# The delta rule's chunks in three streams instead of two, and two places of the array for the last level of the triangular inverses

## The chip, the cores and the metric

The kernel runs on one core of a Trainium2 chip. Its engines take their instructions from queues of their own, each in order: PE (TensorE, matmuls and the weight loads before them), DVE (VectorE), ACT (ScalarE), POOL (GpSimd) and SP, which only issues DMAs here. They meet at semaphores. The metric is the time of one execution on the device, in microseconds (us). All arithmetic is float32; in the trace one matmul of 128 rows shows as two records, a transpose as one.

## What is computed

The reference runs three blocks of a sequence model, one after another, on 512 tokens of width 1024. The change lies in the first block's mixer, and in a helper that the third block also uses. The mixer, cut to what matters:

```python
def chunk_gated_delta_rule(q, k, v, g, beta):
    """S_t = exp(g_t) S_{t-1} (I - beta_t k_t k_t^T) + beta_t k_t v_t^T ; o_t = S_t^T q_t."""
    ...
    m = jnp.where(strict, jnp.einsum("bhncd,bhnmd->bhncm", kb, kc) * decay, 0.0)
    t_sys = jnp.eye(CHUNK, dtype=q.dtype) + m
    u = lax.linalg.triangular_solve(t_sys, vb, left_side=True, lower=True, unit_diagonal=True)
    w = lax.linalg.triangular_solve(t_sys, kb * jnp.exp(gc)[..., None], left_side=True,
                                    lower=True, unit_diagonal=True)
    a_qk = jnp.einsum("bhncd,bhnmd->bhncm", qc, kc) * decay
    def step(state, xs):
        v_new = u_i - jnp.einsum("bhcd,bhde->bhce", w_i, state)
        o_i = ...   # q_i * exp(g_i) @ state + a_i @ v_new
        state = state * jnp.exp(g_last)[..., None, None] + jnp.einsum("bhcd,bhce->bhde", k_dec, v_new)
        return state, o_i
...
o = rms_norm(o, gdn_norm_g) * jax.nn.silu(z.reshape(b, l, GDN_HEADS, GDN_DV))
y_a = o.reshape(b, l, GDN_VW) @ w_gdn_out
```

There are 8 heads of width 128. The third block has an RWKV layer in two directions, which the kernel also computes in chunks with inverses of the same kind.

## The kernel before

The kernel cuts the 512 tokens into `NT = 4` chunks of 128 and handles all 8 heads of a chunk together, in two halves of 4 heads: one PSUM bank holds 4 heads of 128 columns. For each chunk c there are three parts of work.

- The **front**, the first part of `pe_gdn_prepare`, `act_gdn_prepare` and `dve_gdn_prepare`. Six decay matmuls of 512 columns (L1260: `dec`, `eb`, `bb`, for two halves) spread gates over the tile, ScalarE takes their exponentials (L1303), VectorE masks them (L1332 to L1338). Then eight groups of four matmuls or transposes, `gdn kind` 0 to 3 for each half (L1282, L1286), which VectorE takes out with one product each (L1347 to L1353).
- The **inverse** of the unit triangular 128 x 128 matrix of every head (`pe_inverse`, `act_inverse`, `dve_inverse`), by doubling blocks: levels of block size 2 to 32 have a group `inv x` (L833), a transpose `inv t` (L818) that ScalarE copies, and a group `inv y` (L849), each of 16 matmuls of 64 x 64 in all four places of the array; VectorE masks and subtracts (L930, L939). The last level, 64, has an `inv x` of 8 matmuls at one place (L861), 16 transposes by the identity (L869) and an `inv y` of 8 at one place (L878); ScalarE copies all three results (L896, L901, L906). VectorE starts the inverse with four masked products and a subtraction (L914, L919).
- The **steps** (`pe_gdn_steps` and its like), which carry the state from chunk to chunk: `gdn ks` (L1379), two VectorE operations, `gdn vn` (L1391), a copy by ScalarE, `gdn o` (L1402, L1403), `gdn ds` (L1412), and the state's update by VectorE. The second half of the heads stands behind the first.

These parts are generators, and the order of every queue is the order in which a driver advances them. `mixed` puts front and inverse of chunk 0 between the pieces of the conv output gemm (L272, four matmuls a piece), one step for every second piece. `gdn_rounds` then advances `steps(c)` and `prepare(c + 1)` in turn; since an inverse is longer than the steps, most of it stands alone. After the last chunk follow the squares of the output (ScalarE, L1118), the head sums over them (`pe_head_sums`, L628), the first pair of z's gemm (`pe_pair`) and the seven-product steps of z, ga, the output and the mix (`pe_seven`, L348), for which VectorE forms sums of the input (`dve_halves`, L411) and of the weights (L397).

`banks` deals the eight PSUM banks in turn, `weights` the four weight buffers `w0` to `w3` of 1 MB; SP loads a buffer when the last matmul that read it is done. During the delta rule `w0` to `w2` hold the kept tiles of odd chunks and `w3` holds `vn_at` and `R1`, so no weights are loaded there.

The RWKV layer of the third block runs sixteen inverses in `rw_rounds`, each between the work of three other streams.

## Time and profile before

| | us |
|---|---|
| median of 3 runs | 4777.89 |
| lowest, highest | 4777.67, 4782.76 |
| the profiled execution | 4782.63 |
| its span in the trace | 4780.8 |

The profile shows one execution. Its busy times tell how long each engine worked, not what set the end: a wait of an engine counts only where the work behind it is on the chain that ends last. TensorE has two levels of clock, 2.4 GHz (a granted clock of 1.00 in the rows) and 1.2 GHz (0.50); a mean in between is a mix in time. In a timeline a row merges instructions of one line; its duration runs to the end of the last one, which overlaps the next row's start, so from start to start is the better price.

### The profile page before, as it was taken

The numbers are of one execution on the slowest core, as the hardware profiler recorded it, in microseconds if no ns is written. First come the engines' busy times: TensorE is split into PE (matmuls) and PEld (weight loads), VectorE is DVE, ScalarE is ACT, GpSimd is POOL, SyncE is SP. The second block draws the span as 40 slices with busy tenths as digits, with TensorE's granted clock in tenths as the row PEclk, the third lists the DMA queues.
The fourth block names the chain that finished last, engine by engine and source line by source line (L and its number), as shares of the span: only waits on it lengthen the run. The fifth ranks groups of instructions, "written<-read, shape, count | busy, mean of one in ns | idle before, by whom it ended". The sixth has DMA issues, their size and how long they took to land.

```text
span 4780.8 us, 65963 instructions
## 1 busy us (share of the span) xinstructions
PE 4470.1 (94%) x28828; PEld 3314.3 (69%) x28828; DVE 2535.4 (53%) x4388; ACT 824.3 (17%) x1473; POOL 153.9 (3%) x260
## 2 busy tenths in 40 slices
PE   8999998968999899799998999998999988999899
PEld 7887444556878688656655648885888777777644
DVE  5674866333643546546244425555646537777501
ACT  0001012211011100221122210001100014444210
POOL 0000000000000000000000000000000003222100
PEclk9998999967999999899999999998989999999999
DMA  6533452002322222111211122222222210000021
GB/s 240 176 101 58 68 73 53 10 1 56 95 88 80 71 88 82 60 54 36 69 40 36 44 62 90 87 71 88 80 70 89 71 49 2 3 3 2 28 92 44
DMA packets 284958, 311.75 MB, mean 65 GB/s; under 512 B 7168, under 2 KB 277632, under 8 KB 281600
## 3 DMA queue, kind: packets, MB, share of 16 engines
q1 hardware_dynamic: 284672, 307.55, 22.5%
q8 instruction: 227, 3.72, 0.3%
q14 instruction: 59, 0.48, 0.0%
HBM read 305.43 MB, written 2.10 MB: 64 GB/s over the span
## 4 chain that ended last, share of the span: by engine, by line
PE 49%; DVE 4%; ACT 2%; issue 1%; DMA 0%; DVEq 0%; ACTq 0%; SPq 0%
PE ps L348 19%; PE ps L272 13%; PE ps L2940 1%; PE ps L2125 1%; PE ps L317 1%; PE ps L833 1%; PE ps L849 1%; PE ps L818 1%; PE ps L1845 1%; PE ps L2665 1%; PE ps L1834 1%; PE ps L2860 1%; PE ps L2849 0%; PE ps L471 0%; ACT main L901 0%
## 5 line engine op out<-in xcount | busy, mean ns | idle before, releaser
L272 PE MATMUL ps<-main,w 128*128 128x512 f32 (+1 forms) x2832 | 1243.9, 596 | 21.9 <-DMA w<-in_ffn_wg 12.2
L348 PE MATMUL ps<-main 128*128 128x256 f32 x5136 | 1139.2, 379 | 0.0
L348 PEld LDWEIGHTS ps<-main 128*128 128x128 f32 x5136 | 975.5, 190 | 133.1
L272 PEld LDWEIGHTS ps<-main,w 128*128 128x128 f32 x2832 | 543.2, 195 | 647.2 <-issue 619.1
L348 PE MATMUL ps<-main,w 128*128 128x256 f32 x3872 | 863.9, 379 | 1.4 <-DVE main L416 1.4
L348 PEld LDWEIGHTS ps<-main,w 128*128 128x128 f32 x3872 | 736.1, 190 | 105.8 <-issue 4.3
L435 DVE TENSOR_TENSOR main<-main,ps 128x512 f32<-128x512 f32 x164 | 112.8, 688 | 417.7 <-PE ps L348 417.5
L661 DVE SCALAR_TENSOR_TENSOR main<-main,params_sb 128x512 f32<-128x512 f32 x256 | 192.5, 752 | 9.1
L387 ACT COPY main<-ps 128x256 f32<-128x256 f32 x98 | 36.5, 372 | 896.3 <-PE ps L348 896.3
L432 DVE TENSOR_TENSOR main<-main,ps 128x512 f32<-128x512 f32 x98 | 67.3, 687 | 221.2 <-PE ps L348 218.4
L440 DVE TENSOR_TENSOR main<-main,ps 128x512 f32<-128x512 f32 x164 | 112.8, 688 | 78.0 <-PE ps L348 76.7
L397 DVE TENSOR_TENSOR main<-w 128x512 f32<-128x512 f32 (+1 forms) x164 | 111.1, 678 | 31.1 <-DMA w<-in_w_in 12.2
L400 DVE TENSOR_TENSOR main<-main,w 128x512 f32<-128x512 f32 (+1 forms) x164 | 112.4, 685 | 5.7
L402 DVE TENSOR_TENSOR main<-w,main 128x512 f32<-128x512 f32 (+1 forms) x164 | 112.4, 685 | 5.6
L3166 POOL MEMSET w<- 128x512 f32 x128 | 60.8, 526 | 1643.3 <-ACT main L2709 1333.6
L398 DVE TENSOR_TENSOR main<-w 128x512 f32<-128x512 f32 (+1 forms) x164 | 111.1, 677 | 0.0
L387 ACT COPY tmp<-ps 128x256 f32<-128x256 f32 x66 | 24.6, 372 | 498.9 <-PE ps L348 498.9
L2179 DVE TENSOR_TENSOR main<-main 128x512 f32<-128x512 f32 x56 | 38.8, 692 | 135.3 <-PE ps L2125 127.0
L533 ACT ACTIVATE tmp<-main 128x512 f32<-128x512 f32 x104 | 63.8, 629 | 266.2 <-DVE main L585 79.0
L432 DVE TENSOR_TENSOR main<-tmp,ps 128x512 f32<-128x512 f32 x66 | 45.3, 687 | 110.1 <-PE ps L348 109.1
L317 PE MATMUL ps<-w,main 128*128 128x256 f32 (+1 forms) x512 | 101.6, 355 | 0.0
L3092 DVE COPY_PREDICATED w<-consts_sb,ps 128x512 f32<-128x512 uint32 x128 | 85.8, 724 | 27.2 <-PE ps L2940 25.9
(457 smaller groups left out, 4809.7 us busy)
## 6 DMA issues: line engine op xcount, KB each, us to landing
w<-in_w_in SPq DMA_DIRECT2D x58, 1024.0 KB, 6.8
w<-in_e_w_in SPq DMA_DIRECT2D x28, 1024.0 KB, 5.1
main<-in_ada_w SPq DMA_DIRECT2D x24, 1024.0 KB, 5.0
w<-in_ffn_wg SPq DMA_DIRECT2D x22, 1024.0 KB, 6.4
w<-in_ffn_wu SPq DMA_DIRECT2D x22, 1024.0 KB, 6.4
w<-in_o_w_in SPq DMA_DIRECT2D x20, 1024.0 KB, 5.4
w<-in_ffn_wd SPq DMA_DIRECT2D x16, 1024.0 KB, 5.1
w<-in_w_up SPq DMA_DIRECT2D x16, 1024.0 KB, 5.7
```

The source lines that it names most:

```text
L272: i = pe.mm(PS[b][:, 0:n], wv[:, k, f * 128:(f + 1) * 128], g.X(kg + k), start=kg + k == 0, stop=kg + k == g.nk - 1)
L317: i = pe.mm(PS[b][:, 0:m], g.X.ap[:, k, t * 128:(t + 1) * 128], wv[:, k, :], start=k == 0, stop=k == g.nk - 1)
L348: t = pe.mm(PS[b][:, 256 * half:256 * half + 256], weight[:, m, :], x(m), start=m == 0, stop=m == n - 1)
L397: v.tt(S[0], a21, a22, ADD).then_inc(v.inc(s, "sum 0", *step), 1)
L398: v.tt(S[2], a21, a11, SUB).then_inc(v.inc(s, "sum 2", *step), 1)
L400: v.tt(S[1], S[2], a22, ADD).then_inc(v.inc(s, "sum 1", *step), 1)
L402: v.tt(S[3], a12, S[1], SUB).then_inc(v.inc(s, "sums", *step), 1)
L432: v.tt(outer, two(first), b[1], ADD).then_inc(v.inc(s, "out", "seven", 1, *step), 1)
L435: v.tt(inner, two(c[3]), b[2], ADD).then_inc(v.inc(s, "most", *step), 1)
L440: v.tt(inner, inner, b[3], ADD).then_inc(v.inc(s, "out", "seven", 3, *step), 1)
L661: v.stt(out, src[:, j:j + TOK], w(j), out, MUL, ADD).then_inc(v.inc(s, "tap", j, *step), 1)
L3092: v.pick(c3(MS[hd](kind)), mid(const(mask), 4).bitcast(U32), c3(bank("rw ms", i, k))).then_inc(v.inc(s, "out", "rw ms", i, k), 1)
```

## The change

- `gdn_rounds` now drives three streams: the steps of chunk c, the inverse of chunk c + 1 and the front of chunk c + 2 (`together`, `behind`). The halves of the heads in the steps are streams of their own. Rounds: steps 0 with front 1; inverse 1 with front 2; steps 1, inverse 2, front 3; steps 2, inverse 3 and a filler; steps 3.
- The filler is the first pair of z (`pe_pair(pe, G_z, 0)`, slowed by `slowly`) on PE and the input sums (`dve_halves`) on VectorE. `vn_at` and `R1` move out of `w3`, so z's weights can be loaded there early; the tiles of the input sums and of z move too.
- The squares and head sums of a half chunk follow its `gdn o` at once, into a bank held for them (bank 7).
- The inverses' start moves from VectorE to GpSimd (`pool_gdn`).
- Around the conv output gemm, `beside` puts one step of the front behind every third piece and one step of the inverse behind every piece. The kinds of the front come in the order of `g_order`.
- In `pe_inverse` the last `inv x` and `inv y` write to two places in turn, in two banks each; the last transposes are split into a late half (beside `inv x`) and an early half. VectorE copies `inv x` and half of the last `inv y`; ScalarE keeps the rest. This also holds for the RWKV layer.

```diff
@@ drivers @@
+def behind(turns, steps):
+    for _ in range(turns):
+        yield
+    yield from steps
+def together(*streams):
+    streams = list(streams)
+    while streams:
+        streams = [g for g in streams if next(g, "end") != "end"]
+        yield
+def slowly(steps, turns):
+    for _ in steps:
+        for _ in range(turns):
+            yield
+def beside(aside, *parts):
+    for steps, every in parts:
+        for k, _ in enumerate(steps):
+            if k % every == 0:
+                next(aside, None)
     run(aside)
@@ pe_inverse, last level @@
-        for e in range(2):
-            for n in range(4):
-                i = 4 * e + n
-                t = pe.mm(PS[b][late, 64 * i:64 * i + 64], MT[early, i, late], D4[early, n, e, :], start=True, stop=True)
...
-        for i in range(8):
-            for (b, _), h in zip(two, HALF):
-                t = pe.mm(PS[b][h, 64 * i:64 * i + 64], D4[h, i % 4, i // 4, :], ident[h, h], start=True, stop=True)
+        places = late, early
+        for n in range(4):
+            for e in range(2):
+                i = 4 * e + n
+                t = pe.mm(PS[x_banks[e][0]][places[e], 64 * n:64 * n + 64], MT[early, i, late], D4[early, n, e, :],
+                          start=True, stop=True)
+            if n == 3:
+                t.then_inc(pe.inc(s, "mm", "inv x", 64, *name), 1)
+            for e in range(2):
+                i = 4 * e + n
+                t = pe.mm(PS[late_bank][late, 64 * i:64 * i + 64], D4[late, n, e, :], ident[late, late], start=True, stop=True)
...
+        for i in range(8):
+            t = pe.mm(PS[early_bank][early, 64 * i:64 * i + 64], D4[early, i % 4, i // 4, :], ident[early, early],
+                      start=True, stop=True)
...
-        pe.wait_ge(*at("out", "inv t", 64, *name))
-        for i in range(8):
-            t = pe.mm(PS[b][early, 64 * i:64 * i + 64], x[late, 64 * i:64 * i + 64], full[late, i, late], start=True,
-                      stop=True)
+        pe.wait_ge(*at("out", "inv t", 64, "late", *name))
+        places = early, late
+        for n in range(4):
+            for e in range(2):
+                i = 4 * e + n
+                t = pe.mm(PS[y_banks[e][0]][places[e], 64 * n:64 * n + 64], x[late, 64 * i:64 * i + 64], full[late, i, late],
+                          start=True, stop=True)
@@ dve_inverse, last level @@
-        yield
+        v.wait_ge(*at("mm", "inv x", 64, *name))
+        for e, h in enumerate((late, early)):
+            v.move(x[late, 256 * e:256 * e + 256], bank("inv x", 64, e, *name)[h, 0:256]).then_inc(
+                v.inc(s, "out", "inv x", 64, e, *name), 1)
+        v.also("out", "inv x", 64, *name)
+        yield
+        v.wait_ge(*at("mm", "inv y", 64, *name))
+        if free:
+            v.wait_ge(*at(*free))
+        v.ts(full[early, 4:8, late], bank("inv y", 64, 1, *name)[late, 0:256].rearrange("p (i b) -> p i b", b=64), -1.0, None,
+             MUL).then_inc(v.inc(s, "out", "inv y", 64, 1, *name), 1)
@@ delta rule @@
-    vn_at, R1 = wv8[6], wv8[7]
+    vn_at, R1, g_sq = (mem(26864 + 1024 * i, 8, 128) for i in range(3))
+    g_turns = ((0, 1), (3, 4), (2, 5))
+    g_order = [(0, 0), (1, 0), (0, 1), (1, 1), (0, 2), (1, 2), (0, 3), (1, 3)]
+    def pool_gdn(p):
+        s = sem["pool", "gdn"]
+        after(p, "ln1")
+        for c in range(NT):
+            for half in range(2):
+                p.wait_ge(*at("out", "gdn kind", c, half, 0))
+            if c:
+                p.wait_ge(*at("mm", "inv y", 2, "gdn", c - 1))
+            for quarter in QUARTERS:
+                start_blocks(p, s, ("gdn", c), g_mt[c % 2].ap, g_d1, True, [quarter])
+                p.wait_ge(*at("inv first", "pool", "gdn", c))
+            start_inverse(p, s, ("gdn", c), g_d1)
-    def gdn_rounds(e, prepare, steps):
+    def gdn_rounds(e, front, inverse, steps, fill=iter(())):
         after(e, "gdn first")
-        for c in range(NT):
-            for _ in zip_longest(steps(e, c), prepare(e, c + 1) if c < NT - 1 else iter(())):
-                pass
-            e.fence("gdn", c)
+        both = lambda c, late: together(steps(e, c, 0), behind(late, steps(e, c, 1)))
+        run(together(both(0, 0), front(e, 1)))
+        run(together(inverse(e, 1), front(e, 2)))
+        if e.name == "dve":
+            dve_gdn_gate_row(e, 3)
+        run(together(both(1, 0), inverse(e, 2), behind(4, front(e, 3))))
+        if e.name == "pe":
+            banks.only(range(2, 7))
+        run(together(both(2, 0), inverse(e, 3), behind(5 if e.name == "dve" else 3, fill)))
+        run(together(both(3, 0), fill))
         e.fence("gdn")
     def pe_gdn(pe):
         banks.only(range(2, 8))
-        mixed(pe_gdn_prepare(pe, 0), pe_gemm(pe, G_cout), 2)
+        beside(pe_gemm(pe, G_cout), (pe_gdn_front(pe, 0), 3), (pe_gdn_inverse(pe, 0), 1))
...
+        weights.only((3,))
+        gdn_rounds(pe, pe_gdn_front, pe_gdn_inverse, pe_gdn_steps, slowly(pe_pair(pe, G_z, 0), 2))
@@ pe_mixers @@
-        for i in range(8):
-            pe_head_sums(pe, "o1", b, i, t512[i], ("o square", i))
-        run(pe_pair(pe, G_z, 0))
         for g, j in mixer_steps():
...
             run(pe_seven(pe, g, j))
+            if g is G_z and j == 2:
+                weights.only(range(4))
+                input_here("after gdn")
```

How PE's queue changes at the first inverse that stands in the rounds (chunk 1). Before, the end of front 1 and the first levels; L1282 and L1286 are kinds, L818 `inv t`, L833 `inv x`, L849 `inv y`:

```order
L1282 MATMUL ps<-main 128x128 x8
L1286 MATMUL ps<-consts_sb,main 128x128 x8
L818 MATMUL ps<-consts_sb,main 128x128 x4
L833 MATMUL ps<-main 64x64 x16
L849 MATMUL ps<-main 64x64 x16
L833 MATMUL ps<-main 64x64 x16
L818 MATMUL ps<-consts_sb,main 128x128 x4
L849 MATMUL ps<-main 64x64 x16
```

After, the same inverse; L846 is `inv t`, L861 `inv x`, L877 `inv y`, L1299 decay matmuls and L1313 kinds 0 and 1 of front 2:

```order
L846 MATMUL ps<-consts_sb,main 128x128 x4
L1299 MATMUL ps<-main,consts_sb 128x512 x2
L861 MATMUL ps<-main 64x64 x16
L1299 MATMUL ps<-main,consts_sb 128x512 x2
L877 MATMUL ps<-main 64x64 x16
L1330 MATMUL ps<-main,consts_sb 128x8
L1331 MATMUL ps<-main,consts_sb 128x8
L1313 MATMUL ps<-main 128x128 x4
L861 MATMUL ps<-main 64x64 x16
L846 MATMUL ps<-consts_sb,main 128x128 x4
L1313 MATMUL ps<-main 128x128 x4
L877 MATMUL ps<-main 64x64 x16
```

Between every two groups of the inverse now stands a group of front 2. PE's queue in the fourth round (steps 2 done, inverse 3), where L299 is a piece of z's pair in `w3`:

```order
L877 MATMUL ps<-main 64x64 x16
L299 MATMUL ps<-main,w 128x512 x4
L861 MATMUL ps<-main 64x64 x16
L846 MATMUL ps<-consts_sb,main 128x128 x4
L877 MATMUL ps<-main 64x64 x16
L299 MATMUL ps<-main,w 128x512 x4
L861 MATMUL ps<-main 64x64 x16
```

A piece stands behind `inv y`; nothing stands between `inv t` and `inv y`. SP's queue around the end of the delta rule, with what each load waits for: before

```order
L456 DMA w3<-in_w_in 128x8x256 [waits dve_gdn,pe_dense,act_gdn,pe_gdn]
L456 DMA w0<-in_w_in 128x8x256 [waits pe_dense]
L456 DMA w1<-in_w_in 128x8x256 [waits pe_dense]
L456 DMA w2<-in_w_in 128x8x256 [waits pe_dense]
```

and after:

```order
L483 DMA w3<-in_w_in 128x8x256 [waits pe_dense] x2
L483 DMA w3<-in_w_in 128x8x256 [waits dve_gdn,pe_dense,act_gdn,pe_gdn]
L483 DMA w0<-in_w_in 128x8x256
L483 DMA w1<-in_w_in 128x8x256
L483 DMA w2<-in_w_in 128x8x256
```

The first two loads (z's pair and its seven-product step for pair 2) no longer wait for the delta rule; the third is for pair 4 and goes to the same buffer, ahead of the loads to `w0`, `w1` and `w2`.

## Rows read from the trace of the kernel before

**Rows 1.** The profile's page: span, PE's busy time, one DMA row

```profile
span 4780.8 us, 65963 instructions
...
PE 4470.1 (94%) x28828; PEld 3314.3 (69%) x28828; DVE 2535.4 (53%) x4388; ACT 824.3 (17%) x1473; POOL 153.9 (3%) x260
...
w<-in_w_in SPq DMA_DIRECT2D x58, 1024.0 KB, 6.8
```

**Rows 2.** Stretches: length, busy us by engine (x records), granted clock, DMA share, GB/s

```profile
855.50:939.40 83.90, 79.24 (x596) 41.94 (x597) 24.04 (x49) 8.92 (x16) 0.00 (x0) 1.00 0.00 1
939.40:963.50 24.10, 16.86 (x112) 13.41 (x113) 15.95 (x28) 6.00 (x11) 0.00 (x0) 0.93 0.00 0
963.50:994.00 30.50, 21.78 (x405) 18.04 (x405) 5.35 (x21) 4.67 (x8) 0.00 (x0) 0.50 0.01 2
994.00:1027.80 33.80, 23.33 (x145) 18.45 (x145) 18.96 (x32) 6.61 (x12) 0.00 (x0) 0.85 0.00 1
1142.10:1170.30 28.20, 27.53 (x96) 18.94 (x97) 11.61 (x22) 7.65 (x12) 0.00 (x0) 0.76 0.67 150
939.40:1170.30 230.90, 170.89 (x1772) 136.70 (x1773) 83.33 (x179) 43.83 (x76) 0.00 (x0) 0.68 0.09 19
3950.00:4500.00 550.00, 498.29 (x9754) 404.80 (x9758) 412.98 (x1049) 245.59 (x444) 134.90 (x211) 0.98 0.02 4
```

**Rows 3.** PE's timeline, first inverse in the rounds: start, duration, work, [wait, releaser]

```profile
963.52 1.09 PE L818 MATMUL ps<-consts_sb,main 128*128 128x128 f32 x4 [7.15 <-DVE main L919]
...
968.77 1.13 PE L833 MATMUL ps<-main 64*64 64x64 f32 x32 [0.61 <-DVE main L939]
...
971.71 1.14 PE L849 MATMUL ps<-main 64*64 64x64 f32 x32 [0.77 <-ACT main L892]
973.44 1.13 PE L833 MATMUL ps<-main 64*64 64x64 f32 x32 [0.59 <-DVE main L939]
```

**Rows 4.** PE's timeline at full clock: inverse and conv gemm, decays, kinds

```profile
904.43 0.69 PE L833 MATMUL ps<-main 64*64 64x64 f32 x32 [0.61 <-DVE main L939]
905.05 0.66 PE L818 MATMUL ps<-consts_sb,main 128*128 128x128 f32 x4
905.54 3.60 PE L272 MATMUL ps<-main,w 128*128 128x512 f32 x8
...
942.50 1.02 PE L1260 MATMUL ps<-main,consts_sb 128*128 128x512 f32 x2
943.36 1.05 PE L1412 MATMUL ps<-w,main 128*128 128x128 f32 x8
...
953.55 1.95 PE L1282 MATMUL ps<-main 128*128 128x128 f32 x16
955.34 1.04 PE L1286 MATMUL ps<-consts_sb,main 128*128 128x128 f32 x8
```

**Rows 5.** PE's timeline behind the last chunk: head sums, three products

```profile
1142.77 12.27 PE L628 MATMUL ps<-consts_sb,tmp 128*128 128x1 f32 x64 [1.34 <-ACT tmp L1118]
...
1170.33 5.34 PE L348 MATMUL ps<-main,w 128*128 128x256 f32 x24
```

**Rows 6.** DMA issues from 1140 to 1166 us, median us to landing

```profile
w<-in_w_in SPq DMA_DIRECT2D x4, 1024.0 KB, 16.1
```

**Rows 7.** PE's timeline, RWKV stage: column halves in turn, last `inv y`

```profile
4195.89 1.15 PE L2980 MATMUL ps<-main,w 128*64 128x64 f32 x32
...
4200.26 1.11 PE L878 MATMUL ps<-main 64*64 64x64 f32 x16 [0.36 <-ACT main L901]
```

**Rows 8.** VectorE's timeline: inverse's start, a kind's product, a wait

```profile
894.99 1.76 DVE L914 TENSOR_TENSOR main<-main,consts_sb 64x256 f32<-64x256 f32 x4
...
956.10 0.68 DVE L1347 TENSOR_TENSOR main<-ps,main 128x512 f32<-128x512 f32 x1
...
4240.43 0.75 DVE L3103 SCALAR_TENSOR_TENSOR main<-tmp,params_sb,ps 128x512 f32<-128x512 f32 x1 [5.33 <-PE ps L2860]
```

**Rows 9.** GpSimd's timeline: the same start in the RWKV stage

```profile
3945.42 4.39 POOL L914 TENSOR_TENSOR main<-w,consts_sb 64x256 f32<-64x256 f32 x4 [19.66 <-DVE w L3092]
```

More of the change, by code:

```diff
@@ L2 @@
 from contextlib import ExitStack
-from itertools import zip_longest
+from itertools import chain
 import concourse.bass as bass
@@ L1047, in pe_mixers @@
         pe_gdn(pe)
-        b, before = banks.take("head sums", "o1")
-        if before:
-            pe.wait_ge(*at("out", *before))
-        for i in range(8):
-            pe_head_sums(pe, "o1", b, i, t512[i], ("o square", i))
-        run(pe_pair(pe, G_z, 0))
         for g, j in mixer_steps():
@@ L1296, in act_gdn_prepare @@
         if c > 1:
-            after(a, "gdn", c - 2)
-        for half in range(2):
-            hs = slice(4 * half, 4 * half + 4)
-            for which, step, lhs, fn in halves_of:
+            for half in range(2):
+                after(a, "gdn", c - 2, half)
+        for turn in g_turns:
+            for n in turn:
+                half = n // 3
+                hs = slice(4 * half, 4 * half + 4)
+                which, step, lhs, fn = halves_of[n % 3]
                 dst = {"dec": dec, "eb": EB, "bb": BB}[step]
+                if c and step != "eb":
+                    a.wait_ge(*at("out", "gdn kind", c - 1, half, 1))
                 a.wait_ge(*at("mm", "gdn " + step, c, half))
@@ new lines, in dve_gdn_beta_row, with dve_gdn_decays @@
+    def dve_gdn_beta_row(v, c):
+        if c > 1:
+            for half in range(2):
+                after(v, "gdn", c - 2, half)
+        v.wait_ge(*at("beta"))
+        v.tt(g_kept[c % 2][0].ap, bc(be[:, c, :], 128), mid(ident, 8), MUL).then_inc(
+            v.inc(sem["dve", "gdn"], "gdn row", c, 1), 1)
+    def dve_gdn_decays(v, c, half):
+        s, hs = sem["dve", "gdn"], slice(4 * half, 4 * half + 4)
+        v.wait_ge(*at("out", "gdn dec", c, half))
+        v.tt(dec.ap[:, hs, :], dec.ap[:, hs, :], mid(const("le"), 4), MUL).then_inc(v.inc(s, "gdn decay", c, half), 1)
@@ new lines, in act_gdn_steps @@
+    def act_gdn_steps(a, c, half):
+        s = sem["act", "gdn"]
+        ts_ = slice(c * 128, (c + 1) * 128)
+        hs = slice(4 * half, 4 * half + 4)
+        if c:
+            yield
+            a.wait_ge(*at("mm", "gdn o", c - 1, half))
+        a.wait_ge(*at("mm", "gdn vn", c, half))
+        a.copy(vn_at.ap[:, hs, :], c3(bank("gdn vn", c, half))).then_inc(a.inc(s, "out", "gdn vn", c, half), 1)
+        yield
+        a.wait_ge(*at("mm", "gdn o", c, half))
+        a.copy(O1.ap[:, hs, ts_], c3(bank("gdn o", c, half))).then_inc(a.inc(s, "out", "gdn o", c, half), 1)
+        a.fence("gdn", c, half)
+        if c:
+            a.wait_ge(*at("mm", "head sums", "o1", c - 1, half))
+        a.wait_ge(*at("out", "gdn o", c, half))
+        a.act(g_sq.ap[:, hs, :], O1.ap[:, hs, ts_], ACT.Square).then_inc(a.inc(s, "o square", c, half), 1)
+        yield
@@ L1315, in dve_gdn_prepare, with dve_gdn_steps @@
+    def dve_gdn_steps(v, c, half):
         s = sem["dve", "gdn"]
@@ L2872, in dve_shifted @@
         v.stt(out, PP.ap[:, f, o:o + 512], par("o_mu_3", 25 * d + f), out, MUL, ADD).then_inc(v.inc(s, *step), 1)
-    def behind(turns, steps):
-        for _ in range(turns):
-            yield
-        yield from steps
-    def together(*streams):
-        streams = list(streams)
-        while streams:
-            streams = [g for g in streams if next(g, "end") != "end"]
-            yield
     def rw_rounds(e, head, body, inverse, chain, tail, aside):
```

467 lines of the change are left out of this document (246 added, 221 removed).

## Prediction

> **What bounds the kernel now.** I read the page first: TensorE is busy 94% of 4780.8 us [rows 1], so only a stretch where it waits or runs at half clock can give much. The table of stretches shows where that is [rows 2]. From 939.4 to 1170.3 us, the delta rule's rounds and what follows them up to the first seven-product step of z, PE is busy 170.89 of 230.90 us at a granted clock of 0.68; around it the clock is 1.00. The stretch is a chain of phases that stand one after another. 939.4 to 963.5 is steps of chunk 0 with the fronts of chunk 1. 963.5 to 994.0 is an inverse alone. 994.0 to 1027.8 is steps and front again; the pair of phases repeats for the later chunks, the last chunk's steps stand alone, and 1142.1 to 1170.3 is head sums and the first pair of z.
>
> In the PE's timeline the inverse shows why it is slow [rows 3]. It begins after 7.15 us without PE work, in which VectorE works off the products of the front, and the granted clock falls to 0.50 there and stays for the whole inverse. One level, from one `inv x` to the next, takes 4.67 us (968.77 to 973.44), of which the waits for ScalarE's copy and VectorE's subtraction are 0.77 and 0.59. The same groups at full clock take 0.62 and 0.5 us from start to start (904.43 to 905.05 to 905.54) [rows 4]. So the inverse loses twice: nothing lies in its waits, and its matmuls run at 1.2 instead of 2.4 GHz.
>
> **The change, part by part.** *Work that stays.* Prices at full clock, from start to start [rows 4]: a decay matmul takes 0.86 (942.50 to 943.36); a kind 0 or 1 group 0.9 (1.95 for two); a kind 2 or 3 group 0.44 (1.04 for two, with the tail); four matmuls of a dense pair 3.44 (3.60 with overlap). A front is 6 x 0.86 + 0.3 + 4 x 0.9 + 4 x 0.44 = 10.8. An inverse is ten groups of 0.62, five transposes of 0.5, 1.9 for the last `inv x` with its transposes and 0.6 for the last `inv y`: 11.2. The steps of a chunk are groups of 0.9: 5.4 for chunk 0, 9.0 for chunks 1 and 2, 7.2 for the last. The head sums took 12.27 us [rows 5], mostly at half clock (0.76 over 1142.1 to 1170.3) [rows 2]; at full clock I take half, 6.1. The z pair is 4 x 3.44 = 13.8. Together 3 x 10.8 + 3 x 11.2 + 30.6 + 6.1 + 13.8 = 116.5 us of PE work for the stretch that takes 230.9 now.
>
> *What still waits.* I walked the five new rounds in the engines' order, with the hand-offs of rows 3 (about 0.6 us by VectorE, 0.77 by ScalarE) and 0.6 for each VectorE product of 512 columns (0.68 with its overlap) [rows 8]. Round 1 (steps 0 with front 1): the first inverse now starts by GpSimd; its four products take 4.39 us for what VectorE did in 1.76 [rows 8, 9], and with the subtraction I take 5.9 for the start. It begins when both kind 0 products are out of VectorE. PE has issued them after 5.4 of steps, 1.5 of head sums, 5.2 of decays, 0.3 and 1.8, so 14.2 us in; VectorE takes the second out behind two mask products, about 16.5 us into the round, while PE has 4 us of groups left: 22.5 us, 3.5 of it PE waiting. Round 2 (inverse 1 with front 2): each wait of a level has a decay pair or a kind group in it; 21.9 of work, 1.5 of waits: 23.5. Round 3 (steps 1, inverse 2, front 3): 9 + 11.2 + 10.8 + 1.6 of head sums = 32.6 of work, and 3 for the two additions before `gdn vn` and the chunk's copies: 35.5. Round 4 (steps 2, inverse 3, z pair): 9 + 11.2 + 13.8 + 1.6 = 35.6 of work; a chunk of z covers VectorE's wait but nothing stands between transposes and `inv y`, so 5 x 0.77 stay: 40. Round 5 (steps 3 alone): 7.2 + 1.6, and 1.6 of waits: 10.4. Sum 132. The squares and head sums of all but the last chunk, the z pair and the input sums then lie inside these. I add 5 us for orders of VectorE that I did not resolve and for short falls of the clock, as in the later stage of the same build (0.98 over 3950 to 4500 us, PE busy 498 of 550) [rows 2]: 137. **Gain 230.9 - 137 = 94 us.**
>
> *Before the rounds.* 855.5 to 939.4 holds 79.24 of PE work in 83.90 us [rows 2]. With a chunk of the conv gemm behind every step of the inverse, its waits close; the last level now stands uncovered, about 1 us. I take 5 of the 5.7 that the work leaves as **gain 5 us**. GpSimd's start there lies behind three gemm chunks (10 us) and costs nothing; without that cover it would cost 3.
>
> *First seven-product step.* z's weights for pair 2 land in `w3` during the rounds, so the step starts right after the last head sums. But pair 4 now goes to `w3` too, and SP can issue it, and the three behind it, only when pair 2's sixth product is done, some 7 us in (three products take 5.34, so four take 7.1) [rows 5]. Four loads issued together took 16.1 us in the median from issue to landing [rows 6]; this one is first of its four, and the median of all 58 loads of `w_in` is 6.8 [rows 1]. PE wants it 14 us in. At 6.8 it costs nothing, at 16.1 some 9 us; nearest is the single load: **loss 1 us**.
>
> *The last level.* `inv y` 64 has 8 matmuls at one place of the array, 1.11 us for 16 records; in two places at once I take the rate of L2980, which alternates the column halves: 1.15 for 32 records, so 0.67 for 16 with the tail of 0.2 [rows 7]. The last `inv x` with its transposes keeps about 1.9 us, since 16 of the transposes' records stay at one place and then 16 at another. But `inv y` waits 0.36 less [rows 7]: what it needs is copied while the last transposes run. That is 0.8 us in each of 16 inverses of the later RWKV stage, where PE is 91% busy [rows 2]. VectorE gets three more short operations there; it stands idle 5.33 us right at that point, waiting for the PE group behind `inv y` [rows 8], so they are covered; without that cover they would cost about 1 us each round. Two more banks per inverse shift all later banks; bounds from -13 to +5. **Gain 11 us.** The inverses of the delta rule are in their sum above.
>
> L2980 holds all rows of the array in use, alternates only the columns, and runs at 0.03 us a record against 0.06 for L878 [rows 7]; so I take the halved price. A rule speaks against it: the Trainium skill, "TensorE: Matmul & The Clock Gate", Part 3, "The mechanism", says that a weight load overlaps matmuls in flight only when its row group differs. The new `inv y` keeps one row group; by that rule it stays at 1.11 us and the gain here is 4 instead of 11.
>
> **Sum.** 5 + 94 - 1 + 11 = 109. The profiled execution took 4782.6 us, 4.7 over the median of the runs; 4782.6 - 109 = 4673.6, so 4669 for the median.
>
> **The rivals.**
> (a) *VectorE's order takes over.* In rounds 2 and 3 it has 17 and 23 us of work; each of 20 hand-offs of the inverses now stands behind a product of 0.68 that may itself wait for PE. If each costs one: 14 us less gain, 4683. For it: the queue is in order. Against: VectorE is free a quarter to a third of the time, and in the RWKV stage of the same kind PE waits little.
> (b) *The clock stays at half from round 2 on.* In the profile one wait of 7.15 us was followed by the whole phase of 30.5 us at 0.50 [rows 2, 3]. The wait for GpSimd in round 1 is 3.5 us by my walk, and twice that if it starts late. The 98 us of PE work in rounds 2 to 5 would take 98 more, less some 10 of waits that it fills: +88, 4757. Against: the RWKV stage has the same small matmuls among others and keeps 0.98, and here the work is dense.
> (c) *The streams do not overlap.* If a wait of one stream holds the queue of all (the fence on chunk c - 2, a bank still unread), the walls stay and only head sums, z pair and the last level move: about 28 + 5 + 10 gained, 4735. The queue order puts no such wait ahead of its producer, so little for it.
> (d) *Slower.* PE runs at half clock from the conv gemm to the end of z's pair, since small matmuls now stand everywhere between dense chunks. The 79 + 117 us of work would take 392, against 315 before: 109 - 196 = 87 us lost, 4865. It decides from the point where more than 109 of those 196 us of work run at half. Against: the same mix of inverse and gemm runs at 1.00 in 855.5 to 939.4 [rows 2].
> (e) *Two places in one row group don't run at once.* Then the last `inv y` stays at 1.11 us, 0.44 more than I take, in 16 inverses: 7 us less gain, 4676. L2980 speaks against it [rows 7]. (This is what the Trainium skill's rule in "TensorE: Matmul & The Clock Gate", Part 3, would give.)
>
> **How the numbers follow.** Chances: my sum 0.68, (a) 0.14, (b) 0.06, (c) 0.04, (d) 0.01, (e) 0.07. The forecast is 4669. Low end: of the waits only 2 us stay, and none of the 5 that I added (118.5 in place of 137): 4650. High end: (a) with the 9 us of the load and the last level at its bad bound (16 us less) gives 4708; beyond lie (b), (c) and (d), 0.11. Faster by over 0.2% (10 us, about what a measurement of this kernel can tell from no change): 0.98; within: 0.01; slower: 0.01.
>
> **What would show it.** Table of stretches: from the first `gdn vn` to the first seven-product step of z some 137 us at a clock over 0.9, conv gemm stretch 79. A wait of PE on GpSimd's L955 of 2 to 4 us once; PE's level of an inverse near 3.5 us. The last `inv y` at 0.6 to 0.7 us, and the RWKV stretch some 11 us shorter. I am wrong if the clock there is near 0.7, if the largest waits in the rounds are PE on VectorE's products, or if PE waits on the landing of `w3` by over 3 us.

## The result

| | before | after |
|---|---|---|
| median, us | 4778.11 (4 runs) | 4705.45 (4 runs) |
| lowest, highest | 4777.67, 4782.76 | 4703.34, 4711.52 |
| span of the profiled execution | 4780.8 | 4703.3 |

The ratio is 0.9845 with a 95% interval of 0.9833 to 0.9856: the change gains 73 us. The prediction was 4669, a gain of 109 from the median; the time lies in its range, near the high end, 36 us above the forecast.

The profile's page of the changed kernel (compare [rows 1]): PE is busy 45 us less, and the products that read weights now wait 5.3 us for a landing of `w_in`.

```profile
span 4703.3 us, 66069 instructions
...
PE 4425.1 (94%) x28828; PEld 3272.7 (70%) x28828; DVE 2557.4 (54%) x4444; ACT 808.2 (17%) x1453; POOL 171.0 (4%) x280
...
L375 PE MATMUL ps<-main,w 128*128 128x256 f32 x3872 | 866.0, 380 | 6.7 <-DMA w<-in_w_in 5.3
...
w<-in_w_in SPq DMA_DIRECT2D x58, 1024.0 KB, 6.3
```

Stretches of the changed kernel, with the columns of [rows 2] (length, busy us of PE, PEld, DVE, ACT, POOL, granted clock, DMA share, GB/s). First the conv gemm; the five rounds one by one and together, up to z's first seven-product step; the steps of z and ga behind it; a later stage that no edit touches; and the RWKV layer from the first to the last L3105, the PE group that stands behind the last `inv x` of every round (L2983 before).

```profile
855.56:936.27 80.71, 78.84 (x596) 41.21 (x597) 25.00 (x52) 8.13 (x15) 4.16 (x5) 1.00 0.07 14
936.27:960.13 23.86, 21.65 (x133) 17.51 (x133) 14.71 (x27) 8.33 (x15) 4.89 (x5) 0.93 0.00 1
960.13:986.50 26.37, 23.88 (x465) 18.10 (x465) 18.03 (x41) 6.67 (x12) 4.19 (x5) 0.94 0.01 2
986.50:1025.86 39.36, 36.43 (x566) 30.07 (x565) 22.86 (x53) 12.12 (x22) 4.17 (x5) 0.96 0.01 2
1025.86:1068.68 42.82, 37.87 (x535) 26.81 (x533) 17.85 (x49) 7.60 (x13) 0.00 (x0) 1.00 0.11 24
1068.68:1079.65 10.97, 9.64 (x84) 9.18 (x81) 3.10 (x5) 3.98 (x7) 0.00 (x0) 1.00 0.03 10
936.27:1079.65 143.38, 129.47 (x1773) 101.67 (x1773) 76.54 (x174) 38.70 (x69) 13.24 (x15) 0.96 0.04 9
1079.65:1193.30 113.65, 108.35 (x520) 95.57 (x520) 60.20 (x95) 15.12 (x21) 0.00 (x0) 0.97 0.46 102
3450.80:3470.67 19.87, 12.51 (x97) 10.85 (x96) 9.15 (x13) 5.63 (x9) 0.00 (x0) 1.00 0.00 0
3870.06:4407.76 537.70, 480.93 (x9512) 389.04 (x9508) 417.90 (x1052) 226.19 (x413) 132.86 (x208) 0.97 0.01 3
```

The last two of these stretches in the kernel before:

```profile
3529.90:3558.80 28.90, 21.53 (x98) 18.76 (x96) 9.25 (x13) 5.63 (x9) 0.00 (x0) 0.57 0.00 0
3958.48:4483.44 524.96, 478.98 (x9513) 389.58 (x9509) 397.20 (x1010) 237.39 (x427) 133.00 (x208) 0.99 0.01 3
```

The rounds take 143.38 us at a clock of 0.96, where the kernel before took 230.90 at 0.68 [rows 2]. That is the gain, and nearly all of what was forecast. But the RWKV layer, with the same number of PE records within one, takes 12.7 us more. And 9.0 us of the whole gain lie in a stage that the change does not touch: 3529.9 to 3558.8 before and 3450.8 to 3470.7 after hold the same instructions, once at a clock of 0.57 and once at 1.00.

### The profile page after: what moved, and what is told of

Read it like the earlier page. It is cut to its first block, busy times and chain, and to the rows that moved or that the text cites. A ratio compares the mean times of both kernels' runs of the same rounds, so it can differ in the third digit from the quotient of the medians.

```text
span 4703.3 us, 66069 instructions
## 1 busy us (share of the span) xinstructions
PE 4425.1 (94%) x28828; PEld 3272.7 (70%) x28828; DVE 2557.4 (54%) x4444; ACT 808.2 (17%) x1453; POOL 171.0 (4%) x280
## 4 chain that ended last, share of the span: by engine, by line
PE 50%; DVE 4%; ACT 1%; issue 1%; DMA 0%; DVEq 0%; ACTq 0%; SPq 0%
PE ps L375 20%; PE ps L299 14%; PE ps L2258 1%; PE ps L3062 1%; PE ps L344 1%; PE ps L861 1%; PE ps L846 1%; PE ps L877 1%; PE ps L498 1%; PE ps L1978 1%; PE ps L2798 1%; PE ps L1967 1%; PE ps L2993 1%; PE ps L2982 0%; DVE tmp L3005 0%
## 5 line engine op out<-in xcount | busy, mean ns | idle before, releaser
L299 PE MATMUL ps<-main,w 128*128 128x512 f32 (+1 forms) x2832 | 1242.7, 595 | 22.3 <-DMA w<-in_ffn_wg 12.3
L299 PEld LDWEIGHTS ps<-main,w 128*128 128x128 f32 x2832 | 541.3, 194 | 644.1 <-issue 615.1
L344 PEld LDWEIGHTS ps<-w,main 128*128 128x128 f32 x512 | 91.3, 201 | 14.0 <-issue 4.5
```

What stands on the lines that cost most here:

```text
L299: i = pe.mm(PS[b][:, 0:n], wv[:, k, f * 128:(f + 1) * 128], g.X(kg + k), start=kg + k == 0, stop=kg + k == g.nk - 1)
L344: i = pe.mm(PS[b][:, 0:m], g.X.ap[:, k, t * 128:(t + 1) * 128], wv[:, k, :], start=k == 0, stop=k == g.nk - 1)
```

## Where the time went, stretch by stretch

Each stretch is cut at the same instruction in every kernel: the first `gdn vn`; z's first seven-product step; the first product with ga (L1263, L1223 before); the first and the last L3105; the end. Lengths of before in us, and differences from them for the changed kernel and the ten that I ran (profiled executions).

| kernel | to first vn | rounds | z, ga | stages between | RWKV | rest | span |
|---|---|---|---|---|---|---|---|
| before | 939.4 | 230.9 | 104.8 | 2683.3 | 525.0 | 297.4 | 4780.8 |
| after | -3.1 | -87.5 | +8.7 | -6.5 | +12.7 | -1.8 | -77.5 |
| forecast | -5 | -94 | +1 | 0 | -11 | 0 | -109 |
| rw_add_later | -3.9 | -84.6 | +8.6 | -6.3 | -11.4 | -7.2 | -104.8 |
| rw_x_act | -4.0 | -84.6 | +8.6 | -6.3 | -13.2 | -5.5 | -104.9 |
| rw_old_last | -3.3 | -84.3 | +10.6 | -8.2 | -0.1 | +1.9 | -83.4 |
| z_w0 | -3.0 | -87.6 | +1.8 | -6.3 | +12.8 | -1.8 | -84.1 |
| y_in_turn | -3.7 | -84.2 | +7.4 | -12.6 | -10.4 | -1.3 | -104.8 |
| dve_start | -1.4 | -84.1 | +1.8 | -6.6 | -12.4 | -5.6 | -108.4 |
| best1 | -5.0 | -90.6 | +1.8 | -12.8 | -12.6 | -6.0 | -125.2 |
| gate_only | -4.9 | -90.6 | +8.9 | -6.2 | +9.4 | -1.8 | -85.2 |
| best2 | -4.0 | -90.5 | +1.8 | -12.3 | -11.3 | -7.2 | -123.5 |
| bef_last_x_act | -0.2 | -7.6 | 0.0 | -2.2 | -10.8 | -5.3 | -26.2 |

Read the columns down before you read a row across. "RWKV" has three levels: before's own, 10 to 13 us under it, and 9 to 13 over it; the edits say which. "Stages between" holds no edit of any kernel and still moves by 2 to 13 us. PE's idle time there is 144 to 146 us in all twelve kernels and only its busy time moves (2537 us before, 2531 in the changed kernel, 2525 in best1), for the same instructions: that is the granted clock, as in the stage at 3529.9 above, and a whole time can't be read closer than that. The kernel before itself had medians of 4778.1 to 4782.7 us beside the four groups of runs.

"Rest" is no stage without an edit throughout: it begins with the end of the last RWKV round, whose `inv y` stands behind the last L3105. From there to the next L2993 (L2860 before) it is 17.5 us before, 21.8 in the changed kernel and 15.5 in rw_add_later; behind that point 279.9, 273.7 and 274.7. The lengths of stretches decide below, and the whole times are given beside them.

## The RWKV layer: an addition in VectorE's queue

The timelines of one even and one odd round tell the layer's 12.7 us. In an even round of the changed kernel, the last `inv y` (L917) on PE takes 0.68 us for 16 records and starts right behind L3105; VectorE had copied `inv x` (L981) while PE was in the transposes:

```profile
4006.76 1.09 PE L3105 MATMUL ps<-w,main 128*64 128x128 f32 x16
4007.78 0.68 PE L917 MATMUL ps<-main 64*64 64x64 f32 x16
```

```profile
4005.91 0.87 DVE L981 COPY main<-ps 64x256 f32<-64x256 f32 x2 [0.86 <-PE ps L892]
```

That is the case that the prediction priced: 1.11 and a wait of 0.36 before [rows 7], 0.68 and none now. From the start of L3105 to that of the group behind `inv y` it is 1.64 us, where before had 2.49; the round gains 0.85. In the odd round behind it, PE and then VectorE:

```profile
4039.30 1.09 PE L3105 MATMUL ps<-w,main 128*64 128x128 f32 x16
4042.74 1.12 PE L917 MATMUL ps<-main 64*64 64x64 f32 x16 [2.34 <-issue]
```

```profile
4040.45 0.69 DVE L3272 TENSOR_TENSOR main<-main,ps 128x512 f32<-128x512 f32 x1 [3.44 <-PE ps L3105]
4041.05 0.68 DVE L3439 TENSOR_TENSOR main<-main,ps 128x512 f32<-128x512 f32 x1
4041.76 0.88 DVE L981 COPY main<-ps 64x256 f32<-64x256 f32 x2
```

Here the copies come third. Ahead of them in VectorE's queue stands L3272, the addition of the second direction's own output, which exists in every second round alone. It needs L3105, and L3105 stands on PE behind the last `inv x`. So what `inv y` needs waits for a PE group that it does not depend on, then for L3272, then for L3439, then for the copies' own 0.88. PE waits 2.34 us, the profile names no releaser ("issue"), and the clock falls: L917 takes 1.12. PE's waits in the stretch, after and then before (in total, how often, longest):

```profile
PE ps L917 <- issue: 15.8, 7, 2.3
```

```profile
PE ps L878 <- ACT main L901: 5.0, 14, 0.4
```

Seven times 2.3 us in place of fourteen times 0.36; the eighth odd round ends behind the stretch, with a wait of 2.35. The kernel before already shows the hold, in VectorE's waits over the same stretch (L3150 is the addition there):

```profile
DVE main L3150 <- PE ps L2983: 23.6, 7, 3.4
```

Nothing that PE needed soon stood behind that addition then. Three kernels tell this cause (theory A) from the two extra banks of each inverse (theory B) and from something outside the last level (theory C).

### rw_add_later: the addition one step later

```diff
@@ dve_rw_body @@
         dve_rw_picked(v, i, 3)
         yield
+        yield
         if d == 1:
             v.wait_ge(*at("mm", "rw y own", i))
```

> The changed kernel, with one edit: in the RWKV rounds VectorE does the addition of the second direction's own output (L3272) one step later, behind its two copies of the inverse's last inv x (L981) instead of ahead of them. Theory A (order of VectorE's queue): in every second round the copies stand behind an addition that waits for a PE group issued behind that inv x, so the last inv y waits 2.3 us and the clock falls; without it all sixteen rounds gain 0.85 us as the even ones do. The stretch from the first to the last L3105 falls from 538.5 us to 512 (525.7 less 16 x 0.85), the whole to 4679 us. Theory B (the two extra banks of each inverse make PE wait for a bank that is still unread): banks are the same, so the stretch stays at 538 and the whole at 4705.

Measured: 4677.28 us, ratio 0.9789 (0.9773 to 0.9806), 28 us under the changed kernel; the stretch 513.5 us. Theory A had said 4679 and 512, theory B 4705 and 538. An odd round of it, PE and VectorE; L3273 is the addition, now behind L981 and in nobody's way:

```profile
4036.28 1.09 PE L3105 MATMUL ps<-w,main 128*64 128x128 f32 x16
4037.31 0.68 PE L917 MATMUL ps<-main 64*64 64x64 f32 x16
```

```profile
4035.44 0.88 DVE L981 COPY main<-ps 64x256 f32<-64x256 f32 x2 [0.85 <-PE ps L892]
4037.43 0.69 DVE L3273 TENSOR_TENSOR main<-main,ps 128x512 f32<-128x512 f32 x1 [1.11 <-PE ps L3105]
```

One line of the program and no work taken away: 24.2 us of this stretch, and 6.4 in the end of the last round. The banks are unchanged, so B falls.

### rw_x_act: ScalarE copies the last inv x

```diff
@@ act_inverse, last level, RWKV only @@
+            a.wait_ge(*at("mm", "inv x", 64, *name))
+            for e, h in enumerate((late, early)):
+                a.copy(x[late, 256 * e:256 * e + 256], bank("inv x", 64, e, *name)[h, 0:256]).then_inc(
+                    a.inc(s, "out", "inv x", 64, e, *name), 1)
...
@@ dve_inverse, last level, RWKV only @@
-        v.wait_ge(*at("mm", "inv x", 64, *name))
-        for e, h in enumerate((late, early)):
-            v.move(x[late, 256 * e:256 * e + 256], bank("inv x", 64, e, *name)[h, 0:256]).then_inc(
...
```

> The changed kernel, but in the RWKV layer ScalarE copies both halves of the last inv x, ahead of its copies of the transposes, and VectorE does not. Two places, four banks and VectorE's addition stay as they are. Theory A (order of VectorE's queue): the 2.3 us before every second inv y go; ScalarE now has three or four copies in a row, so some 0.3 to 0.7 us of wait before inv y appear in all sixteen rounds: the stretch 517 to 523 us, the whole 4684 to 4690. Theory B (banks): stretch 538, whole 4705.

Measured: 4676.76 us, ratio 0.9787 (0.9772 to 0.9801); the stretch 511.8. A holds again by another way, and better than I had expected: I had 0.3 to 0.7 us of wait before each `inv y`, and there is none. ScalarE's timeline in an odd round shows why: both copies of `inv x` take 0.76 together, and the first of the two transposes' copies, the one that `inv y` needs, is out before L917 begins at 4036.83.

```profile
4034.96 0.76 ACT L937 COPY main<-ps 64x256 f32<-64x256 f32 x2 [0.29 <-PE ps L892]
4035.74 1.19 ACT L944 COPY main<-ps 64x512 f32<-64x512 f32 x2
```

### rw_old_last: the last level of before, RWKV only

`pe_inverse`, `act_inverse` and `dve_inverse` take before's last level when they are called for the RWKV layer, and the new one in the delta rule.

> The changed kernel with the last level of the inverse of before in the RWKV layer alone (one place, one bank each, ScalarE copies all three); the delta rule keeps everything new. Theories A and B both: the stretch from the first to the last L3105 comes back from 538.5 to the 525.7 us of before, and the whole to 4692. Theory C (the stage is slower for a reason outside the last level, as the clock or what the stages ahead left behind): the stretch stays near 538 and the whole at 4705.

Measured: 4697.23 us, ratio 0.983 (0.9815 to 0.9844); the stretch 524.8 where before had 525.0. So all of the loss and all of the gain in this layer are the last level's; theory C falls. The whole lies 5 us above my 4692. Beside rw_add_later its z is 2 us longer in code that is the same; of the 9 us in "rest", 2.2 lie in the end of the last round, which has the old last level, and 7 behind it, in code that is the same.

### y_in_turn: are two places at work at once?

The prediction's rival (e) said that places in one row group don't run at once. This kernel (on top of rw_x_act) keeps places, banks and copies, and only orders the eight matmuls of the last `inv y` otherwise:

```diff
-        for n in range(4):
-            for e in range(2):
+        for e in range(2):
+            for n in range(4):
```

> The changed kernel with ScalarE's copy in the RWKV layer, and in both kinds of inverses the last inv y does four matmuls at one place and then four at the other, in place of alternating; places, banks and copies are the same. Against 4676.8 of that kernel with alternation: by my theory (two column places at work at once, though both use the same rows of the array) it takes 1.0 us and not 0.68, in 16 inverses: 4682. By the rule that matmuls of one row group don't overlap anyhow, alternation gave nothing and the time stays at 4677, the group at 0.68.

Measured: 4680.31 us, ratio 0.9788 (0.9773 to 0.9803), the stretch 514.5. PE's row of the group with alternation (rw_x_act) and without:

```profile
4004.28 0.68 PE L917 MATMUL ps<-main 64*64 64x64 f32 x16
```

```profile
3998.05 0.96 PE L917 MATMUL ps<-main 64*64 64x64 f32 x16
```

0.68 against 0.96: the 16 records are alike, all on the same rows of the array. Alternation is worth 0.28 us a group. The two places in turn are still 0.15 faster than the single one of before [rows 7], since even then they overlap: the trace's single records start 0.058 us apart at one place, and the second place's first starts 0.29 us into the group, before the first place's last at 0.46. The wholes differ by 3.6, but the kernel before differed by 3.5 beside the two runs and the ratios are equal, so only the rows and the stretch (2.7 us) show it. Rival (e) falls. So does, here, the rule as the prediction read it from the Trainium skill ("TensorE: Matmul & The Clock Gate", Part 3, "The mechanism"), by which a weight load overlaps matmuls in flight only where the row group differs. What the Trainium skill says in "TensorEngine Tiling (Array Packing)", "Key Properties", that different tiles can do their loads and matmuls in parallel, agrees with these two rows.

### bef_last_x_act: the new last level alone, on the kernel before

> The kernel before with nothing but the new last level of the inverse (in delta rule and RWKV layer), where ScalarE copies both halves of the last inv x. If the last level's own gain is what the prediction said (0.8 us in each of 16 inverses, the price of 1.11 against 0.68 and the wait), the RWKV stretch falls from 525.0 to 512 to 514 and the whole by 12 to 14 us, to 4766. If the gain of the RWKV stretch in the other runs came from the new delta rule or from a luckier clock, it stays near 4779.

Measured: 4755.6 us against 4782.74, ratio 0.9945 (0.9928 to 0.9961), 27 us. The RWKV stretch falls to 514.1, as expected. The end of the last round gives 2.0 more (15.5 for 17.5), so the layer gains what I had said. Some 13 us I had not expected. 7.6 lie in the old rounds, whose inverses stand alone: PE's idle time there falls by 4.1 and its busy time by 3.5 (I had priced these three inverses at nothing). 5.6 lie in stages that the edit does not touch. So the whole of 27 us can't be credited to the edit.

## The first steps of z

PE's timeline of the changed kernel, and SP's issue of the four loads:

```profile
1079.65 7.11 PE L375 MATMUL ps<-main,w 128*128 128x256 f32 x24
...
1100.75 2.50 PE L375 MATMUL ps<-main,w 128*128 128x256 f32 x5 [5.30 <-DMA w<-in_w_in]
```

```profile
1088.58 13.06 SPq L483 DMA_DIRECT2D w<-in_w_in  x4
```

The load of pair 4 goes out when pair 2 has left `w3`, 8.9 us into the step, and has landed 12.2 us later; PE waits 5.30. The step itself begins slowly (7.11 where three products take 5.34 [rows 5]) and so does the one behind the wait (6.84): 3.3 us more at half clock. The first of these 1.8 us stands ahead of the wait and is not the load's.

### z_w0: pair 4 in w0

```diff
             if g is G_z and j == 2:
                 weights.only(range(4))
+                weights.i[0, 1, 2, 3] = 0
```

> The changed kernel, but the weights for z's pair 4 go to w0 (free with the delta rule) and not to w3 (free only when pair 2 is done); the other three follow in w1, w2, w3. Theory D (the turn of the buffers): PE's wait of 5.3 us for that load goes and with it the stretch at half clock behind it, 7 us in all; the whole 4698. Theory E (three loads are issued at once then and share the engines, so that the first lands after 14 us): a wait of 2 us or more stays and the whole is 4701 to 4705.

Measured: 4700.93 us, ratio 0.9836 (0.9822 to 0.9851); 4.5 us less in the medians, 6.6 in the span, 6.9 in the stretch "z, ga". The loads go out at once behind the last head sums and the wait is gone, with the half clock behind it; the slow 7.11 ahead of it stays:

```profile
1093.62 1.95 PE L679 MATMUL ps<-consts_sb,small 128*128 128x128 f32 x16
1095.40 5.35 PE L375 MATMUL ps<-main,w 128*128 128x256 f32 x24
```

```profile
1079.93 12.90 SPq L483 DMA_DIRECT2D w<-in_w_in  x4
```

Theory D holds. Theory E was not idle: the median of the four from issue to landing is 16.9 us, but the first was there in the 15.5 us that PE left it.

## The first round

Two waits of PE stand out in the rounds of the changed kernel: 1.86 us before the first `gdn vn`, and 2.21 before the first transpose of inverse 1, each with slow rows behind it. The second one's releaser is shown as a VectorE row; GpSimd's start of the inverse ended at the same instant (954.78 to 959.98):

```profile
936.27 3.65 PE L1495 MATMUL ps<-main 128*128 128x128 f32 x16 [1.86 <-DVE main L1372]
...
960.13 0.98 PE L846 MATMUL ps<-consts_sb,main 128*128 128x128 f32 x4 [2.21 <-DVE w L1449]
```

```profile
954.78 3.46 POOL L950 TENSOR_TENSOR main<-main,consts_sb 64x256 f32<-64x256 f32 x4 [79.30 <-DVE main L1410]
958.32 1.66 POOL L955 TENSOR_TENSOR main<-consts_sb,main 128x512 f32<-128x512 f32 x1
```

### gate_only: the mark ahead of the gate row

```diff
-        dve_gdn_gate_row(v, 1)
         v.fence("gdn first")
+        dve_gdn_gate_row(v, 1)
```

The first `gdn vn` does not need the gate row of chunk 1, but all engines begin the rounds at the mark that VectorE sets behind it.

> The changed kernel with one edit: VectorE sets the mark that lets the rounds begin before it forms the gate row of chunk 1. In the run with three edits the first gdn vn came 2.0 us sooner and the stretch up to z's first seven-product step was 3.1 us shorter than with two of them, and its whole came out 8 us under the sum of the edits. If the edit itself is worth 5 us and the rest was the granted clock of other stages, here the two stretches give 5 us together and the whole falls to 4700, give or take the 6 us by which the unchanged stages have differed between kernels. If the gain of 13 us belongs to the edit by a way I do not see, it is 4692 with a gain inside the rounds or right behind them.

Measured: 4695.6 us, ratio 0.9821 (0.9805 to 0.9838): 10 us under the changed kernel, of which the two stretches hold 1.8 and 3.0, as expected, and the RWKV stretch 3.4 that the edit doesn't reach: PE's idle time there is 56.7 us as in the changed kernel's 56.8, its busy time 3.3 less. So the edit is worth 5 us, and what best1 gained beyond its edits was clock.

### dve_start: VectorE starts the inverses

```diff
@@ dve_gdn_front, behind the second kind 0 @@
+            if n == 1:
...
+                if c:
+                    v.wait_ge(*at("mm", "inv y", 2, "gdn", c - 1))
+                start_blocks(v, s, ("gdn", c), g_mt[c % 2].ap, g_d1, True, QUARTERS)
+                v.wait_ge(*at("inv first", "dve", "gdn", c))
+                start_inverse(v, s, ("gdn", c), g_d1)
@@ pool_gdn: nothing is left in it @@
```

> ScalarE's copy in the RWKV layer and w0 for pair 4 as in the run beside it, the mark where the changed kernel has it; and the start of the delta rule's inverses goes back from GpSimd to VectorE, right behind its second product of kind 0 in the front. The prediction priced GpSimd's start with 3.5 us of waiting by PE in the first round. If GpSimd's time is what PE waits for there, the wait of 2.2 us before the first transpose of inverse 1 and the half clock behind it (1.5 us) go, while VectorE has 2.5 us more in each of three rounds: 4669 (less 3). If VectorE's queue is what binds the rounds, as rival (a) said, those 2.5 us show as PE waits in rounds 2 and 3 and the whole is 4675 (more 3).

Measured: 4672.78 us, ratio 0.9772 (0.9757 to 0.9786). Its base (ScalarE's copy and w0) was not run by itself; by the stretches and medians of the two single kernels it would stand at 4670 to 4672. Its first `gdn vn` is 1.6 us later than z_w0's and its rounds are 146.8 us, against 143.4 and 146.4 of the two. The whole leaves it open, but the waits do not: within the rounds PE waits 16.7 us, and 13.9 in each of the other two. The 2.21 before the first transpose is gone; 0.77, 1.49 and 0.39 stand near it instead, and the same `inv x` of rounds 2 and 3 waits 1.70 for VectorE's subtraction, where it had 0.51 and nothing. So VectorE's start costs 2.9 us of waits, as the second expectation said, and GpSimd's is the better one here; that the whole shows little of it is the granted clock of the rounds (0.97, and 0.94 in rw_x_act).

### best1 and best2

best1 is rw_x_act, z_w0 and the mark ahead of the gate row; best2 has the addition one step later in place of ScalarE's copies.

> Three edits on the changed kernel: ScalarE copies the RWKV layer's last inv x, z's pair 4 takes w0, and VectorE sets the mark that lets the rounds begin before it forms the gate row of chunk 1 (L1372, 1.2 us) and not after. By the theory of VectorE's queue the first gdn vn waited 1.86 us for that mark and ran at half clock after it (3.65 us for two groups that take 1.95): with the row behind the mark the stretch from the first vn to z's first seven-product step keeps its length less 1.7 and begins 1.2 us sooner, 3 us in all, so the whole is 4677 - 5 - 3 = 4669. If the first vn waits for something else (its own copies), it stays at 4672.

> Three edits on the changed kernel: VectorE's addition L3272 behind its copies of the last inv x in the RWKV rounds (in place of ScalarE's copies), z's pair 4 in w0, and the mark ahead of the gate row. By the stretches of the single runs: 4705.5 - 26 (RWKV) - 7 (load) - 5 (mark) = 4667, and as low as 4658 if the clock of the unchanged stages falls as in the run with ScalarE's copies. If the edits do not add up, since PE reaches other waits sooner, it stays above 4675.

Measured: best1 4658.41 us, ratio 0.9744 (0.9729 to 0.9758); best2 4661.6, ratio 0.9757 (0.9743 to 0.9772). Both beat the changed kernel by over 40 us, and the edits add up. Stretch by stretch best1 against the changed kernel: 1.9 sooner, 3.1 in the rounds, 6.9 in z, 25.3 in RWKV and 6.2 in the end of the last round, 43 in all of 47.7; the rest is clock in stages without an edit. Its first `gdn vn`, to be held against the row at 936.27:

```profile
934.40 2.02 PE L1503 MATMUL ps<-main 128*128 128x128 f32 x16 [0.73 <-DVE main L995]
```

## Why the prediction came out as it did

**The rounds (forecast 94 less, measured 87.5): right in kind, one term short.** All five rounds run at 0.93 to 1.00, and no round is an inverse alone. Rivals (b), (c) and (d) fall. Against my walk: 23.9 (22.5), 26.4 (23.5), 39.4 (35.5), 42.8 (40), 11.0 (10.4). The waits that the timeline shows within the rounds sum to 13.9 us, where the walk had 15.5; the clock costs 4.8 (each length times what its clock lacks of 1), where I had added 5. The term that was mis-sized is the first one, the work: 143.4 - 13.9 - 4.8 = 124.7 us at full clock, where I had 116.5. I took prices of groups that stand behind one of their own kind, 0.9 for a kind of four heads from 1.95 for two. In the new order each stands between groups of another kind, from round 2:

```profile
967.72 1.14 PE L1313 MATMUL ps<-main 128*128 128x128 f32 x8
968.79 0.69 PE L861 MATMUL ps<-main 64*64 64x64 f32 x32
969.42 0.66 PE L846 MATMUL ps<-consts_sb,main 128*128 128x128 f32 x4
969.91 1.06 PE L1313 MATMUL ps<-main 128*128 128x128 f32 x8
971.51 0.69 PE L877 MATMUL ps<-main 64*64 64x64 f32 x32 [0.55 <-DVE main L967]
```

967.72 to 968.79 is 1.07 us for a kind 0 group. The same kernel's round 1 holds the other case: there front 1's kinds stand one behind the other, and they come at the prediction's prices, 3.65 us for the four groups of kinds 0 and 1 (3.6) and 1.75 for the four of kinds 2 and 3 (1.76):

```profile
950.64 3.82 PE L1313 MATMUL ps<-main 128*128 128x128 f32 x32
954.29 1.91 PE L1317 MATMUL ps<-consts_sb,main 128*128 128x128 f32 x16
```

In round 2 the same eight groups take 4.19 and 2.51, waits taken off. And rounds 4 and 5 ran at a clock of 1.00, so no clock enters there: PE's work is 42.8 and 11.0 less waits of 4.9 and 1.3, that is 37.9 and 9.6, where I had 35.6 and 8.8. So 3.1 of the 8.2 us are shown without any clock in them, and in round 2 the kinds account for 1.3 more. How the rest splits into neighbours, tails ahead of waits and the head sums (1.9 us a chunk, where I had 1.6) is open; no run changed the order alone. Four waits of 0.77 for ScalarE's copy came in round 4, where the walk had five. Rival (a) did not come: PE waits for VectorE's products and additions ten times in the five rounds, 0.5 to 1.1 us each, 6.7 in all; its largest wait for VectorE, ahead of the first `gdn vn`, is for the mark. The wait for GpSimd, 3.5 in the text, was 2.21. The walk's own figures give 4.8 for it (22.5 less 17.7 of work), and two decay groups of front 2 (1.9 us), which the queue puts ahead of that wait, cover some of it.

**Before the rounds (5, measured 3.1).** The work was right (78.84 us in 80.71). The step that failed is one I did not take: among the orders of VectorE I did not see that the mark stands behind the gate row. With gate_only it is 4.9 here, and the rounds are 3 shorter.

**z's load (1, measured 8.7).** The step "nearest is the single load", 6.8 us, failed: it took 12.2 from an issue at 8.9 us, not 7. Of the 8.7 us, 5.3 are the wait and 1.5 the half clock behind it; 1.8 are the slow start of z's first step, which z_w0 keeps. "PE waits on the landing of w3 by over 3 us" was on my list of signs, and it was so.

**The last level (11 less, measured 12.7 more).** The price was right: 11.4 and 13.2 us in the two kernels where nothing stands in the way. (16 times 0.8 is 12.8; the prediction wrote 11 and gave no reason for the difference.) The step that failed is "VectorE gets three more short operations there; it stands idle 5.33 us right at that point ... so they are covered". I read one idle time in one round, of a queue that differs between even and odd rounds, and asked whether VectorE had time, not what stood ahead of the copies. The 5.33 us belong to an even round, which has no addition; the odd rounds' wait of 3.4 us ahead of the addition was in the same trace. This is most of the 36 us: 24 of them, and the end of the last round, 4.3 longer than before, comes on top. The term's bad bound was 5 us more, given for the banks; the measured 12.7 more lies well outside it.

**What no step spoke of, and luck.** "Stages between" and "rest" gave 8.3 us. Without the end of the last RWKV round, which lost 4.3, it is 12.6 us in stages that no edit touches, 9.0 of them in the one that ran at 0.57 before. No step of the prediction earned them, and without even the 8.3 the time would be near 4714, beyond the high end of 4708. That end was added up from rival (a), the load at its worst and the last level at its bad bound; (a) did not come, the load nearly did, and the last level went past its bound. That the time lies in the range is in part luck.

In sum: 109 - 6.5 (rounds) - 1.9 (before them) - 7.7 (z) - 23.7 (RWKV) + 8.3 (stages between and rest) = 77.5, the difference of the spans. The medians differ by 5 less, since the profiled execution of before lay 4.7 over its median.

## What to carry to other kernels

When work moves to an engine that "has time", list what stands ahead of it in that engine's queue in every kind of round, and for each of those what it waits for. If one of them waits for work that the waiting engine does only just before it needs your result, the idle time is no cover. A step of order can be as good a cure as another engine: one `yield` gave 28 us of 4705, ScalarE's copies 29, and a mark set one instruction earlier gave 5. And where an interleaving breaks up groups of one kind, price each at the start-to-start time between strangers.

## What the runs showed of the hardware

- The granted clock falls behind waits of very different length, and not behind all of them: the 1.86 us before the first `gdn vn` was followed by 3.65 us for work that takes 2.02, behind the wait of 5.30 the next step began with 6.84 in place of 5.35, and behind the same wait of 2.21 in round 1 four transposes took 0.98 in the changed kernel, 1.09 in rw_add_later and 0.63 in best1. The same rounds ran at 0.96 (143.4 us) in two kernels and at 0.94 (146.3) in rw_add_later, whose code there is the same:

```profile
935.51:1081.84 146.33, 132.41 (x1773) 102.66 (x1773) 76.58 (x174) 38.71 (x69) 13.23 (x15) 0.94 0.04 9
```

- Stages without any edit (2683 us before) differ by up to 13 us between kernels in PE's busy time, with its idle time the same within 2 us. For effects below that, compare stretches.
- Two column places of the array on the same rows work at the same time when matmuls alternate between them, for 64 x 64 float32: 16 records take 0.68 us, 0.96 with the places in turn, and 1.11 at one place.
- A group of four 128 x 128 float32 matmuls took 0.91 us from start to start among its own kind (round 1) and 0.98 to 1.09 between other groups (round 2).
